# Routing tokens to experts by matmuls with selection matrices, four experts to a block, in a decoder step on one core

## The reference

```
h = x + (g_a * (o_a @ w_proj_a) + g_b * (o_b @ w_proj_b)) @ w_out
t = rmsnorm(h)                                   # 264 x 1024
group  = top-1 of 4 by softmax(t @ w_rg + b_rg)
e1, e2 = top-2 of the group's 8 experts          # weights wt_1, wt_2 from softmax, times the group's
y[n]   = sum over the token's two experts e of
         wt_e * ( silu(t[n] @ w_gate[e]) * (t[n] @ w_up[e]) ) @ w_down[e]     # 32 experts, D_EXPERT = 256
out = rmsnorm_final(h + y)
```

## Time and profile before

| | us |
|---|---|
| median of 3 runs | 826.6 |
| lowest, highest | 822.04, 829.06 |
| the profiled execution | 832.18 |
| its span, first to last instruction | 830.3 |

### The profile page before, as it was taken

How to read it: one execution, slowest core, us unless ns; L and a number is a source line. 1 busy time by engine, 2 the same in 40 slices (tenths; PEclk the granted TensorE clock), 3 DMA queues, 4 the chain that set the end, 5 groups by cost and what they waited for, 6 DMA issues and landing times.

```text
span 830.3 us, 7873 instructions
## 1 busy us (share of the span) xinstructions
PE 629.7 (76%) x3108; PEld 356.3 (43%) x3108; DVE 314.2 (38%) x490; ACT 149.9 (18%) x282; POOL 129.1 (16%) x119
## 2 busy tenths in 40 slices
PE   4969898997997898766899861586777877778710
PEld 3856764676885455325774251121222222222200
DVE  3079998987899870320230155000000000000005
ACT  2124033324104515330000100110110101101101
POOL 2434222111115352111000003100000000000020
PEclk9998899999999796987799955598998899989965
DMA  9997899588657889577789010199999999999631
GB/s 339 413 411 275 313 382 409 198 322 325 242 193 262 318 294 402 204 293 298 273 325 396 34 52 0 52 350 396 399 398 402 400 394 398 400 403 398 261 128 57
DMA packets 123916, 245.12 MB, mean 295 GB/s; under 512 B 14163, under 2 KB 86371, under 8 KB 113612
## 3 DMA queue, kind: packets, MB, share of 16 engines
q1 hardware_dynamic: 103932, 140.33, 46.0%
q0 software_dynamic: 14832, 94.98, 29.7%
q10 hardware_dynamic: 5120, 9.37, 3.1%
HBM read 232.66 MB, written 12.00 MB: 295 GB/s over the span
## 4 chain that ended last, share of the span: by engine, by line
PE 36%; SPq 23%; DVE 16%; DMA 9%; ACT 6%; issue 6%; POOL 2%; ACTq 1%; POOLq 0%; DVEq 0%
SPq L443 19%; PE PS L603 8%; PE PS L1030 5%; SPq L446 4%; DVE arena L1473 4%; PE PS L1021 4%; DVE x_rows L1477 4%; PE PS L1076 4%; PE PS L947 2%; DMA arena<-in_w_proj_b 2%; PE PS L1094 2%; DMA temp<-in_cache_k_a,page_idx 2%; PE PS L724 2%; DMA arena<-in_w_up 1%; PE PS L883 1%
## 5 line engine op out<-in xcount | busy, mean ns | idle before, releaser
L1076 PE MATMUL PS<-arena,temp 128*32 128x512 f32 x512 | 138.1, 701 | 37.4 <-DMA arena<-in_w_up 36.0
L603 PE MATMUL PS<-xT,arena 128*128 128x264 f32 x608 | 142.7, 394 | 4.6 <-ACT arena L1271 4.2
L603 PEld LDWEIGHTS PS<-xT,arena 128*128 128x128 f32 x608 | 116.2, 194 | 26.1 <-ACT arena L1271 4.8
L1877 DVE TENSOR_TENSOR temp<-PS,temp 64x256 f32<-64x256 f32 x16 | 6.8, 422 | 266.5 <-ACT temp L1390 266.5
L1076 PEld LDWEIGHTS PS<-arena,temp 128*32 128x32 f32 x512 | 39.5, 125 | 132.4 <-issue 132.4
L1473 DVE TENSOR_TENSOR arena<-arena,x_rows 128x2048 f32<-128x2048 f32 x32 | 73.0, 2283 | 28.8 <-DMA x_rows<-q_dram 28.7
L1477 DVE TENSOR_REDUCE x_rows<-arena 128x32 f32<-128x2048 f32 x32 | 73.2, 2288 | 1.1
L1094 PE MATMUL PS<-arena,temp 128*32 128x512 f32 x256 | 58.0, 594 | 12.3 <-ACT temp L1394 12.3
L503 POOL DMA_INDIRECT arena<-in_cache_k_b,unit_idx x32 | 39.5, 1234 | 147.5 <-DVE x_rows L1477 142.5
L503 POOL DMA_INDIRECT arena<-in_cache_v_b,unit_idx x32 | 37.6, 1176 | 78.4 <-PE PS L947 57.8
L503 POOL DMA_INDIRECT temp<-x_dram,slot_tok x9 | 8.6, 958 | 225.2 <-PE PS L1103 223.7
(11 more groups left out here) (319 smaller groups left out, 722.1 us busy)
## 6 DMA issues: line engine op xcount, KB each, us to landing
arena<-in_w_gate SPq DMA_DIRECT2D x32, 1024.0 KB, 11.6
arena<-in_w_up SPq DMA_DIRECT2D x32, 1024.0 KB, 12.0
arena<-in_w_down SPq DMA_DIRECT2D x32, 1024.0 KB, 11.2
arena<-in_w_in SPq DMA_DIRECT2D x9, 2048.0 KB, 11.3
temp<-in_w_out SPq DMA_DIRECT2D x1, 4096.0 KB, 15.3
y_dram<-temp ACTq DMA_DIRECT2D x8, 512.0 KB, 6.5
x_rows<-in_x_prompt SPq DMA_DIRECT2D x2, 1024.0 KB
bias_dram<-x_rows SPq DMA_DIRECT2D x1, 2048.0 KB, 18.0
```

Source lines behind the costliest of these rows:

```text
L603: last = nc.tensor.matmul(PS[0:m, n % 2, 0:T], w[:, k, c0:c0 + m], xT[:, k, :], start=(k == 0), stop=(k == KC - 1))
L1076: last = nc.tensor.matmul(PS[k * CAP:(k + 1) * CAP, 2 + n, :], xgT[:, d, k * CAP:(k + 1) * CAP], slots[k][:, d * 2 * DE:(d + 1) * 2 * DE], ...
```

## The change

Nothing of the experts' traffic but their weights goes through DRAM any more.

- **Into the experts.** DVE builds for each quad a 0/1 matrix `into` (tokens x 128 slots) by comparing a row of slot numbers with each token's two rows, `quad_row`, from which 128 is taken off from quad to quad. `collect` multiplies `x2_rows` by it on PE: for each of 8 chunks and 3 token tiles one matmul of 128 columns, 24 in a quad. The outcome is at once the transposed `xgT`. The gathers, `x2_dram`, `table_dram`, the scatters, `slot_tok`, `tok_i` and the zero writes go, and with them SP's wait for `s_zero`.
- **Back.** `back` is the same matrix with the weights in place of ones; PE transposes it (three transposes a quad), ACT copies it to `backT`. `combine(j)`, six matmuls of 512 columns a quad, multiplies it with `y_sb` in the next quad (after the loop for the last one), and DVE adds each to `x_rows`. `y_dram`, its writes and the last gathers go.
- **Four at once.** The gate/up matmuls of all four experts run in four column groups, and so do the down matmuls; silu, the product and the transposes run once a quad instead of twice. SP waits for the block of all four before it reloads any of the slots.
- **The end.** The final sum, squares and scaling are interleaved by token tile.

The core of the diff, left-out parts marked by dots:

```diff
             sp.wait_ge(s_proj, N_KB)
             sp.dma_start(w_b[:, :, :], w_in[:, :, O_KB + 512:O_KB + 1024]).then_inc(s_wb, 16)
-            sp.dma_start(y_dram[NE * CAP:QUAD * NQX, :].rearrange("(p j) (k n) -> p (j k) n", p=P, n=P),
-                         const("zeros").unsqueeze(1).to_broadcast([P, NOVF * CAP * D // P // P, P])).then_inc(s_yout, 16)
...
-            sp.dma_start(tok_i[:, :], a["token_ids"]).then_inc(s_tokid, 16)
-            sp.wait_ge(s_zero, 1)
-            sp.dma_start(table_dram.rearrange("(p t) o -> p (t o)", p=QUAD), zero_i[:, :]).then_inc(s_tokz, 16)
...
             with sp.Fori(1, NQ) as i:
-                for n in range(2):
-                    sp.wait_ge(s_gu, i * 2 + (n - 1))
-                    for k in (2 * n, 2 * n + 1):
-                        gate_up(bass.ds(i * 4 + k, 1), k)
-                    sp.wait_ge(s_down, i * 2 + (n - 1))
-                    for k in (2 * n, 2 * n + 1):
-                        down(bass.ds(i * 4 + k, 1), k)
+                sp.wait_ge(s_gu, i)
+                for k in range(4):
+                    gate_up(bass.ds(i * 4 + k, 1), k)
+                sp.wait_ge(s_down, i * 2)
+                for k in range(4):
+                    down(bass.ds(i * 4 + k, 1), k)
...
+            def collect(i):
+
+                pe.wait_ge(s_into, i + 1)
+                for c in range(KC):
+                    for t, (_, n) in enumerate(TILES):
+                        last = nc.tensor.matmul(PS[:, c // 4, c % 4 * QUAD:(c % 4 + 1) * QUAD], x2_rows[0:n, t, c:D:KC],
+                                                into[0:n, t, :], start=(t == 0), stop=(t == 2))
+                last.then_inc(s_gtr, 1)
+
+            def combine(j):
+                t, half = j // 2, j % 2
+                t0, n = TILES[t]
+                return nc.tensor.matmul(PS[0:n, ACC + 2 + half, :], backT[:, t0:t0 + n], y_sb[:, half, :],
+                                        start=True, stop=True)
+
+            def quad(i):
+
+                pe.wait_ge(s_gT, i + 1)
+                for k in range(4):
                     pe.wait_ge(s_we[k], i * 32 + 32)
                 for d in range(KC):
-                    for k in experts:
-                        last = nc.tensor.matmul(PS[k * CAP:(k + 1) * CAP, 2 + n, :], xgT[:, d, k * CAP:(k + 1) * CAP],
+                    for k in range(4):
+                        last = nc.tensor.matmul(PS[k * CAP:(k + 1) * CAP, 2, :], xgT[:, d, k * CAP:(k + 1) * CAP],
                                                 slots[k][:, d * 2 * DE:(d + 1) * 2 * DE],
                                                 start=(d == 0), stop=(d == KC - 1))
                 last.then_inc(s_gu, 1)
+                if not isinstance(i, int) or i:
+                    for j in range(6):
+                        if j >= 2:
+                            pe.wait_ge(s_add, i * 6 + (j - 7))
+                        combine(j).then_inc(s_comb, 1)
+                pe.wait_ge(s_back, i + 1)
+                for t, (t0, n) in enumerate(TILES):
+                    last = nc.tensor.transpose(PS[:, 3, t0:t0 + n], back[0:n, t, :], ident[0:n, 0:n])
+                last.then_inc(s_bt, 1)
+                if not isinstance(i, int) or i < NQX - 1:
+                    collect(i + 1)
+
+                pe.wait_ge(s_hid, i + 1)
...
+                pe.wait_ge(s_btc, i + 1)
+                pe.wait_ge(s_y0, i + 1)
+                pe.wait_ge(s_y1, i + 1)
+                if not isinstance(i, int) or i:
+                    pe.wait_ge(s_add, i * 6)
+
+            collect(0)
+            quad(0)
+            with pe.Fori(1, NQ) as i:
                 quad(i)
...
+            for j in range(6):
+                if j >= 2:
+                    pe.wait_ge(s_fadd, j - 1)
+                combine(j).then_inc(s_fcomb, 1)
```

ScalarE's order in a quad, and VectorE's:

```diff
+                act.wait_ge(s_gu, i + 1)
+                nc.scalar.activation(act_e, PS[:, 2, 0:DE], ACT.Silu).then_inc(s_act, 1)
+                act.wait_ge(s_bt, i + 1)
+                nc.scalar.copy(backT, PS[:, 3, 0:T]).then_inc(s_btc, 1)
+                if not isinstance(i, int) or i < NQX - 1:
+                    collected(i + 1)
+                act.wait_ge(s_hT, i + 1)
+                nc.scalar.copy(hidT, PS[:, 2, 0:2 * P].rearrange("p (f m) -> p f m", f=2)).then_inc(s_hTc, 1)
+                act.wait_ge(s_down, i * 2 + 1)
+                nc.scalar.copy(y_sb[:, 0, :], PS[:, ACC, :]).then_inc(s_y0, 1)
...
+                if more:
+                    dve.wait_ge(s_gtr, i + 1)
+                    nc.vector.tensor_scalar(quad_row[:, :, :], quad_row[:, :, :], -float(QUAD), None, ALU.add
+                                            ).then_inc(s_step, 1)
+                    dve.wait_ge(s_step, i * STEPS + (STEPS + 1))
+                    slots_in(i + 1)
+                dve.wait_ge(s_act, i + 1)
+                nc.vector.tensor_tensor(hid, PS[:, 2, DE:2 * DE], act_e, ALU.mult).then_inc(s_hid, 1)
+                if not isinstance(i, int) or i:
+                    for j in range(6):
+                        dve.wait_ge(s_comb, i * 6 + (j - 5))
+                        add(j, s_add)
+                if more:
+                    dve.wait_ge(s_bt, i + 1)
+                    slots_back(i + 1)
+                dve.wait_ge(s_down, i * 2 + 2)
+                nc.vector.tensor_copy(y_sb[:, 1, :], PS[:, ACC + 1, :]).then_inc(s_y1, 1)
```

More of the change, by code:

```diff
@@ L1079, in two_experts @@
                 last.then_inc(s_gu, 1)
-                if n == 1 and not (isinstance(i, int) and i == NQX - 1):
-                    turn(i + 1)
-                pe.wait_ge(s_hid, i * 2 + (n + 1))
+                if not isinstance(i, int) or i:
[10 more added lines that the diff above has]
+                pe.wait_ge(s_hid, i + 1)
                 for f in range(2):
-                    last = nc.tensor.transpose(PS[:, ACC + 2, f * P:(f + 1) * P], hid[:, f * P:(f + 1) * P], ident)
+                    last = nc.tensor.transpose(PS[:, 2, f * P:(f + 1) * P], hid[:, f * P:(f + 1) * P], ident)
                 last.then_inc(s_hT, 1)
-                pe.wait_ge(s_hTc, i * 2 + (n + 1))
-                for k in experts:
+                pe.wait_ge(s_hTc, i + 1)
+                for k in range(4):
                     pe.wait_ge(s_wd[k], i * 16 + 16)
@@ L1385, in quad @@
             def quad(i):
[L1387 to L1401 removed]
+                act.wait_ge(s_gu, i + 1)
[8 more added lines that the diff above has]
+                nc.scalar.copy(y_sb[:, 0, :], PS[:, ACC, :]).then_inc(s_y0, 1)
             act.wait_ge(s_x2T, 5)
[L1404 removed]
+            collected(0)
             act.preload_act_table(ACT.Silu)
@@ L1869, in _, with add @@
             nc.vector.tensor_copy(ovf_i[0:1, 1:NOVF + 1], blk).then_inc(s_ovf, 1)
-            def quad(i):
-                for n in range(2):
-                    rows = slice(2 * n * CAP, 2 * (n + 1) * CAP)
-                    u = PS[rows, 2 + n, DE:2 * DE]
-                    dve.wait_ge(s_act, i * 2 + (n + 1))
-                    nc.vector.tensor_tensor(hid[rows, :], u, act_e[rows, :], ALU.mult).then_inc(s_hid, 1)
-            link(nc.vector.memset(hid, 0.0))
-            with dve.Fori(0, NQ) as i:
+            def add(j, added):
+                t, half = j // 2, j % 2
+                n, cols = TILES[t][1], slice(half * 512, (half + 1) * 512)
+                nc.vector.tensor_tensor(x_rows[0:n, t, cols], PS[0:n, ACC + 2 + half, :], x_rows[0:n, t, cols], ALU.add
+                                        ).then_inc(added, 1)
+            def quad(i):
+                more = not isinstance(i, int) or i < NQX - 1
+                if more:
[15 more added lines that the diff above has]
+                nc.vector.tensor_copy(y_sb[:, 1, :], PS[:, ACC + 1, :]).then_inc(s_y1, 1)
+            quad(0)
+            with dve.Fori(1, NQ) as i:
                 quad(i)
```

211 lines of the change are left out of this document (86 added, 125 removed).

## The result

The kernel became slower. The median of four runs of the changed kernel is 857.7 us (855.5 to 864.3), against 824.8 us for the kernel before on the same chip (four runs, 822.0 to 829.1): ratio 1.041, 95% interval 1.033 to 1.048. The profiled execution took 864.3 us; its span is 862.5 us, 32.2 more than the 830.3 of before.

A forecast was written before the change was run, and what follows sets the result against it. The prediction took the DMA stream of expert weights to bound the stage. Its terms, -2.5 + 0.5 - 8.8 - 9.0 - 4.9 = -24.7 us, gave 802 us from the median 826.6, 3% less, with a range of 786 to 822.

The forecast's parts named there:

- last reduce to first block: Start of the expert stage: copy and small operations 2.0, `collect(0)` 8.5, copy and hops 1.3; 11.8 us, gain 8.8.
- first to last block: Expert loop: 32.4 us for the first round, then six of 34.4, together 238.8 against 247.75; gain 9.0.
- last block to the end: Tail from the start of the last gate/up block: 47.7 us with hops against 52.6; gain 4.9.
- the cover of 6 us: In a round, TensorE's chain to `y_sb` ends at 27.5 us; next down loads' turn comes at 33.
- rival D: Expert rounds: TensorE's chain, not the stream, sets them; 47 us all at 1.2 GHz, total near 890 us; chance 0.10.
- Four branches: Tail, before the last combines: reading the overflow count and four branches, 2.1 us.
- order of w_proj: Ahead of the stage: earlier `w_proj` slows the last `v_a` gathers; 0.5 us lost (2.1 gained to 2.6 lost).
- The zero write: Far ahead of the stage: dropping the 2 MB zeroing of `y_dram` gains 2.5 us (nothing to 5.1).
- the pause: Each round, the weight stream stands dry for 2.6 us until the gate/up block of four experts frees the slots.
- The shorter round by the Trainium skill's fixed cost: Expert reloads: each of seven 1.5 us shorter by the page's DMA fixed cost, some 10 us; not in the sum.
- A: The main forecast: expert rounds of 34.4 us, total time 802 us, range 790 to 813; chance 0.60.
- rival B: Expert rounds: stream's stop nearly vanishes (0.6 us), gate/up block 7.0 us or quicker reload, rounds 32.4, total 790 us; chance 0.12.

The follow-up runs named there:

- contiguous tiles: Changed kernel with collect() taking 128 neighbouring columns of x2_rows instead of every eighth: 822.7 us; with gate/up weights loaded in matching row order, 826.2 us.
- single jump: Changed kernel with the four conditional overflow rounds inside one more condition on TensorE, ScalarE and VectorE: 852.7 us, ratio 1.033 to the kernel before.
- both repairs: Changed kernel with `into` stationary and x2_rows moving in the gather, plus the four overflow rounds inside one condition: 813.1 us, ratio 0.980 to the kernel before.
- the form with the rows moving: Changed kernel with `into` stationary and x2_rows moving, six matmuls of 512 columns, then eight transposes: 819.3 us, ratio 0.990 to the kernel before.
- the clock held up: Rows-moving gather and one overflow condition, plus seven unread 128x512 matmuls before the next gate/up block: 802.8 us, ratio 0.969 to the kernel before.

## Why the prediction was wrong

The forecast was 802 us, 3% faster; it became 4% slower. The sum was -24.7 us on the span, the measured difference +32.2: a miss of 56.9 us.

| step | forecast | after | miss |
|---|---|---|---|
| up to the routing's last reduce | 509.3 - 2.0 = 507.3 | 512.0 | +4.7 |
| last reduce to first block | 11.8 | 531.24 - 511.99 = 19.3 | +7.5 |
| first to last block | 238.8 | 791.96 - 531.24 = 260.7 | +21.9 |
| last block to the end | 47.7 | 862.5 - 791.96 = 70.5 | +22.8 |

**The failed step is the price of a record of `collect`.** The text took 0.14 us from the transposes, with 0.145 and 0.244 as bounds "(all warm, all cold)", and called the cover of 6 us safe at both. The bounds spanned the clock; the real question was whether a two-record float32 matmul with a strided stationary operand is like a transpose at all. It is not: 0.33 us. That is +9.1 us in each round and +9.2 in the tail, where `collect` still runs ahead of the conditional rounds. Even contiguous it costs 0.177, and 0.31 at the lower clock, so the upper bound was too low there too. The contiguous tiles brought back 36 us by that one edit. (The lower bound of 6.4 us isn't 48 x 0.145 either, which is 7.0; nothing hangs on it.)

**At the start of the stage the clock was wrong, not only the stride.** `collect(0)` is 7.7 us over the forecast, and contiguous tiles take only 1.2 us of that away. The forecast had the first 4 us at the lower clock and the rest at the higher; no row shows that, and the clock stayed at 0.50 for the whole of it with either tiles. With six matmuls of 512 columns in its place it rose: the gather there takes 7.9 us, at 0.95 on average in its second half. The first block, priced at 7.0 with the clock up, took 9.14 for the same reason.

**With that price the cover is gone, and rival D's mechanism decides.** TensorE's chain after the block was put at 5.2 + 0.5 + 6.7 + 1.6 + 3.7 and 0.8 to `y_sb`; it measures 5.64, 0.52, 15.76, 1.66, 5.35 and 0.7, and 1.0 of issue. With the block the round is 37.75 us. D had named 34.4 us as the point where it binds and 38 as the one where it turns the sign. The round stayed just short of 38, and the loop's 21.9 us alone would not have turned it: the start and the tail did the rest. TensorE's chain came to bind not by a clock at 1.2 GHz throughout, as written, but by the loads, and the lower clock came with them (0.50 for 16 us of the round, the down matmuls 5.35 us, where 3.64 is what they take at 1.00 with contiguous tiles). D had 0.10, because its price was worked out only for the clock.

**The second failed step is the branches.** "Four branches" were priced at 2.1 us by what GpSimd shows for its own. GpSimd's conditional blocks are short; TensorE's hold a whole round. The stretch measured 15.3 us, 13.2 more. The single jump took 10.6 of it away. That the length of the block skipped makes the price is argued, not shown: no run varied it.

**The small edits.** The order of w_proj: sign right (a loss), 3.5 us measured where 0.5 stood and 2.6 was the bound. Its mechanism was right: the last `v_a` gather lands later (396.2 against 391.8 in the earlier trace rows) because w_proj shares the stream. The zero write stays open, as told above. The table's first row, +4.7 us, is in any case smaller than the 10 us by which that part scatters.

**What held.** Once the gather is fast enough, the round is the forecast's: 34.15 us for 34.4, the pause 2.5 for 2.6, at the place named, the block 9.2 to 9.6 us in the last five rounds (8.5 to 10.1 over all) for 9.0. The shorter round by the Trainium skill's fixed cost, cited beside it (DMA: Bandwidth & Descriptors, section "Anatomy of one DMA"), was not borne out; that section is on DMAs issued by GpSimd, while SyncE issues these loads. With both repairs, first to last block is 240.9 us for 238.8, and from the last block to the end 812.5 - 763.62 = 48.9 for 47.7. But this is the form with the rows moving. In the forecast's own order of work, with contiguous tiles, rounds average 33.2 us, the block takes 7.1 to 9.6, and 232.6 us pass from the first block to the last, 6 less than forecast: part of the way from A to rival B. In the changed kernel the block was warm (7.07), as rival B had it, because TensorE idled for less than 2 us before it; the stream had no use for it.

The kernel as changed thus had a gain of 2% in it (0.980 with two repairs that alter no transfer), 2.5% with the order of w_proj left alone as well, and 3% with the clock held up instead of that.

## What to carry to other kernels

Lay the stationary operand of a float32 matmul out so that neighbouring elements are at most 8 bytes apart, or make the other operand the stationary one; a stride of four elements made the whole instruction take almost twice as long here while the clock was at 2.4 GHz. When an operation isn't in the trace, let the bounds span what differs between it and its nearest row (operand pattern, passes, operation), not only the clock, and ask what the cover is worth at twice the price. Put rarely taken rounds behind a single condition: each skip over one cost 2 to 4 us on TensorE here.

## What the runs showed of the hardware that was not expected

- A weight load of 128 columns in a float32 matmul: 0.188 us contiguous at 2.4 GHz and 0.333 at 1.2 GHz; with 32 bytes from element to element 0.332 at either. A record of the matmul with it goes from 0.177 us (contiguous, 2.4 GHz) to 0.33; at 1.2 GHz it is 0.314 contiguous and 0.34 strided. In a transpose a load with the same stride took 0.193 us.
- While TensorE ran these slow loads back to back, its granted clock fell from 1.00 to 0.50, 4 us after they began, and came back during the down matmuls some 17 us later; with contiguous tiles in the same place it stayed at 1.00 through `collect` (in one round it was at 0.50 for a while behind it, from 620 to 622 us). A strided record of `collect` costs 0.32 to 0.34 us at either level, but the matmuls behind it pay for the lower one. In `collect(0)` the records show PE busy for 15 us in a row with the granted clock at 0.50 throughout, contiguous or not.
- A skip over a conditional block as large as a round takes 3.5 to 3.8 us on TensorE (2.2 in one pair of kernels), with one packet of 16 KB on the instruction queue; four in a row took 14.4 to 15.3 us in the kernels that collect by columns and 11.3 in the one that moves the rows. With seven matmuls just ahead of the jump the stretch of issue was gone from the chain, but they took 6.0 us themselves.
- Profiles of kernels that are alike up to 350 us differ by up to 10 us in when the values begin (359.6 to 369.8), which is more than most single edits here are worth. The interval from there to the first matmul with w_proj repeats within 0.6 us over eleven profiles.
